# Keeping the residual stream token-major, and multiplying the output weights as the moving operand

## The reference, cut to what matters

```python
h = h + rmsnorm(mixer(rmsnorm(h, g0)), g1)          # layers 0 and 1
h = h + rmsnorm(conv_ffn(rmsnorm(h, g2)), g3)
x = x + 0.5 * swiglu(rms_norm(x, n1))                # second block
x = x + concat(mla, moba) @ w_out                    # on rms_norm(x, n2)
x = x + 0.5 * swiglu(rms_norm(x, n3))
return rms_norm(x, final)

def rmsnorm(x, g):
    return x * rsqrt(mean(x * x, axis=-1) + 1e-6) * g
def conv_ffn(x, w_up, conv_w, conv_b, w_down):
    h = causal_dwconv(x @ w_up, conv_w, conv_b)      # 2 x 2816 channels
    return (gelu(h[..., :2816]) * h[..., 2816:]) @ w_down
```

## Time and profile before

| | before |
|---|---|
| median of three runs | 1165.03 us |
| span of the profiled execution | 1165.7 us |
| TensorE busy (matmul) | 1113.5 us, 96% |
| TensorE weight load busy | 1084.9 us, 93% |
| VectorE busy | 810.1 us, 69% |
| ScalarE busy | 621.9 us, 53% |
| GpSimd busy | 68.5 us, 6% |
| read from HBM | 188.58 MB, 164 GB/s over the span |

### The profile page before, as it was taken

The page is one execution under the profiler, slowest core; times in us unless marked ns, Lnnn a source line. Parts: engine busy times, 40 slices in busy tenths (PEclk is TensorE's granted clock), DMA queues, the critical chain, the costliest instruction groups (busy, mean ns, idle before and its releaser), DMA issues.

```text
span 1165.7 us, 23900 instructions
## 1 busy us (share of the span) xinstructions
PE 1113.5 (96%) x8840; PEld 1084.9 (93%) x8840; DVE 810.1 (69%) x1245; ACT 621.9 (53%) x1048; POOL 68.5 (6%) x79
## 2 busy tenths in 40 slices
PE   6798999999899889999998999999999999999996
PEld 5698999999799889999998999999999999999995
DVE  5587887776858768877777755655766868656554
ACT  5455655555646656655555644444554656444442
POOL 0077000000200001000001000000000000000000
PEclk9899999999999999999999999999999999999998
DMA  9763565555353243655554465565552435565630
GB/s 335 151 227 113 167 212 180 180 180 180 106 181 129 91 163 99 212 180 193 180 180 146 147 191 186 172 190 178 160 165 92 152 113 171 184 194 165 193 111 36
DMA packets 54033, 191.91 MB, mean 165 GB/s; under 512 B 6504, under 2 KB 6920, under 8 KB 53984
## 3 DMA queue, kind: packets, MB, share of 16 engines
q1 hardware_dynamic: 52272, 187.96, 49.5%
q0 software_dynamic: 1088, 2.63, 1.4%
q10 hardware_dynamic: 624, 0.64, 0.2%
HBM read 188.58 MB, written 2.62 MB: 164 GB/s over the span
## 4 chain that ended last, share of the span: by engine, by line
PE 87%; DVE 6%; DMA 4%; ACT 2%; issue 1%; POOL 0%; SPq 0%; DVEq 0%; ACTq 0%; POOLq 0%
PE G L1127 18%; PE G L1128 18%; PE G L1129 18%; PE Y L1127 8%; PE Y L1129 8%; PE Y L1128 8%; DMA raw<-in_panels 4%; DVE w_low L666 1%; PE PB L1144 1%; PE Y L1185 1%; PE Y L1187 1%; PE Y L1186 1%; ACT w_high L349 1%; PE PB L1290 1%; DVE rbc L677 1%
## 5 line engine op out<-in xcount | busy, mean ns | idle before, releaser
L1127 PE MATMUL G<-x_high,w_high 128*128 128x256 f32 x1712 | 489.1, 286 | 8.8 <-DVE x_low L684 8.8
L1128 PE MATMUL G<-x_low,w_high 128*128 128x256 f32 x1712 | 485.8, 284 | 0.0
L1129 PE MATMUL G<-x_high,w_low 128*128 128x256 f32 x1712 | 485.7, 284 | 0.0
L666 DVE TENSOR_TENSOR w_low<-raw,w_high 128x1024 fp32r<-128x1024 f32 x352 | 428.1, 1225 | 57.3 <-ACT w_high L349 56.8
L349 ACT CAST w_high<-raw 128x1024 fp32r<-128x1024 f32 x352 | 363.3, 1042 | 94.6 <-PE G L1129 65.5
L1127 PEld LDWEIGHTS G<-x_high,w_high 128*128 128x128 f32 x1712 | 329.9, 193 | 11.1 <-issue 9.6
L1128 PEld LDWEIGHTS G<-x_low,w_high 128*128 128x128 f32 x1712 | 330.0, 193 | 0.2
L1129 PEld LDWEIGHTS G<-x_high,w_low 128*128 128x128 f32 x1712 | 330.0, 193 | 0.0
L1127 PE MATMUL Y<-a_high,w_high 128*128 128x256 f32 x896 | 255.5, 285 | 0.0
L1128 PE MATMUL Y<-a_low,w_high 128*128 128x256 f32 x896 | 254.2, 284 | 0.0
L1129 PE MATMUL Y<-a_high,w_low 128*128 128x256 f32 x896 | 254.1, 284 | 0.0
(11 more groups left out here) (201 smaller groups left out, 889.5 us busy)
## 6 DMA issues: line engine op xcount, KB each, us to landing
raw<-in_panels SPq DMA_DIRECT2D x352, 512.0 KB, 3.7
rel_rows<-qk POOLq DMA_DIRECT2D x1, 1536.0 KB, 34.9
h<-in_x SPq DMA_DIRECT2D x4, 256.0 KB, 10.1
bias<-rel_rows POOLq DMA_DIRECT2D x8, 128.0 KB, 4.4
out_y<-big SPq DMA_DIRECT2D x4, 256.0 KB, 2.0
big<-in_w_s SPq DMA_DIRECT2D x1, 512.0 KB, 12.5
wc<-in_b_s SPq DMA_DIRECT2D x1, 512.0 KB, 13.9
cst<-in_consts ACTq DMA_DIRECT2D x1, 320.5 KB, 5.5
```

Of the source, the lines that this page charges most:

```text
L666: v.tensor_tensor(WL[:, j, :], raw[:, j, :], WH[:, j, :].bitcast(F32), ALU.subtract).then_inc(lo, 1)
L1127: mm(out, WH[:, j, c:c + w], xh, start=first, stop=False, skip_group_check=skip)
L1128: mm(out, WH[:, j, c:c + w], xl, start=False, stop=False, skip_group_check=skip)
L1129: return mm(out, WL[:, j, c:c + w], xh, start=False, stop=last, skip_group_check=skip)
```

## The change

The kernel is written anew around another layout. What it does:

1. `h`, the stage's output and all norms are token-major: 128 tokens on the partitions and 1024 features side by side, for token tile 0 and token tile 1. The sum of squares of a token is then one pass of ScalarE with its accumulator, and the reciprocal root is one number on each partition. The sums with a matrix of ones (1144) are gone, and so is the multiplication of the tiles by the norm (`rbc`), since x is normalised before it is used. The gains are rows now, spread over the partitions by DMAs: one of 512 KB at each boundary, two at boundaries 1 to 4.
2. x has to be turned back to feature-major for the products. TensorE transposes it in 128 x 128 blocks, 16 at each of the stages' starts (`turn_x`), ScalarE and VectorE write the high and low part from there.
3. An output panel keeps a 128-token block of the hidden activations stationary and moves 512 weight columns (`rows`): 12 matmuls, six for each token tile.
4. The last five output panels of a stage (`tail`) serve token tile 0 first, save that one part of tile 1 is put in; the boundary's work on tile 0 begins while TensorE still works on tile 1 of the other four.
5. The first four feature tiles of a stage (`first_tiles`, boundaries 1, 3, 4, 5 and 6) are computed for token tile 0 and then for token tile 1, with 128 moving columns each. The first value panels (the start and boundary 2) serve tile 0, then tile 1, with 512 moving columns as before.
6. The raw ring has five buffers, that of high and low parts eight. Six matmuls without use (`warm`) stand before `turn_x` at each of boundaries 1 to 6. The loops are unrolled. In feed-forward stages the accumulator banks of the gate and up tiles are four instead of two, and the convolution reads them there.
7. At the start, the LayerNorm statistics of token tile 1 and the offset are computed behind more panel splits, the mixing comes at the seventh panel of the second product instead of the fifth, and the DMAs that read the attention bias back come later.

```diff
-RING = 6
+RAWS = 5
+RING = 8
-            def rows_into_y(n, j, xh, xl, first, last):
-                ready(n)
-                for k in range(KT):
-                    end = product(Y[:, k, :], j, k * P, P, xh, xl, first and k % 2 == 0, last, skip=True)
+            def rows(n, slot, t, first, last):
+                ready(n)
+                j = n % RING
+                xh, xl = AH[:, slot, tok(t)], AL[:, slot, tok(t)]
+                for x, w, start, stop in ((xh, WH, first, False), (xl, WH, False, False), (xh, WL, False, last)):
+                    for c in range(2):
+                        end = mm(Y[:, 2 * t + c, :], x, w[:, j, half(c)], start=start, stop=stop)
+                if t == 1:
+                    end.then_inc(used, 1)
...
+            def turn_x(b, t):
+                for c in range(2):
+                    pe.wait_ge(xn_r, quarter(b, t, c))
+                    for j in range(4):
+                        last = nc.tensor.transpose(Y[:, 2 * t + c, j * P:(j + 1) * P],
+                                                   xn[:, t, (4 * c + j) * P:(4 * c + j + 1) * P], ident)
+                    last.then_inc(xt_r, 1)
+            def tail(end, slots, before=None):
...
+                for i in range(4):
+                    part(i, 0)
+                part(0, 1)
+                part(4, 0).then_inc(y_done, 1)
+                for i in range(1, 4):
+                    part(i, 1)
+                part(4, 1)
+            def first_tiles(b, outs):
+                n = STARTS[b]
+                turn_x(b, 0)
+                for m in range(3):
+                    tile_part(b, n + m, outs[m], 0)
+                turn_x(b, 1)
+                tile_part(b, n + 3, outs[3], 0)
+                for m in range(4):
+                    tile_part(b, n + m, outs[m], 1)
```

The boundary on VectorE, for boundaries 1 to 4 and for the others:

```diff
+                if b in POST:
+                    y_scale(b, 0)
+                    link(y_normed(b, 0, 0))
+                    link(y_normed(b, 0, 1))
+                    h_add(0, 0), h_add(0, 1)
+                    half_mean(b, 0)
+                    upto(base + 4)
+                    x_normed(b, 0)
+                    y_scale(b, 1)
+                    link(y_normed(b, 1, 0))
+                    x_low(b, 0, 0)
+                    link(y_normed(b, 1, 1))
+                    x_low(b, 0, 1)
+                    h_add(1, 0), h_add(1, 1)
+                elif b:
+                    h_plus_y(b, 0)
+                    half_mean(b, 0)
+                    x_normed(b, 0)
+                    if b < 7:
+                        x_low(b, 0, 0), x_low(b, 0, 1)
+                    h_plus_y(b, 1)
+                half_mean(b, 1)
+                x_normed(b, 1)
```

More of the change, by code:

```diff
@@ L42 @@
 REL = 384
[L45 removed]
+WARM = 6
 GMLP = 0
@@ L269, in _ @@
+            for t in range(TT):
+                for c in range(2):
+                    sp.wait_ge(out_r, 2 * t + c + 1)
+                    sp.dma_start(io["out"][tok(t), half(c)], xn[:, t, half(c)]).then_inc(out_sem, 16)
             sp.wait_ge(out_sem, 64)
@@ L432, in ffn @@
+                if not conv:
+                    gap(2)
+                gap(1)
             def ffn(ph, base, with_conv):
-                def static(f):
-                    def split_next(c):
-                        if 6 < 3 * f + c and base + 3 * f + c < PANELS:
-                            splits(base + 3 * f + c, base + 3 * f + c)
+                for f in range(NF):
                     c0 = C_CONV + (ph * NF + f) * 8
-                    hidden(f % 2, ph * NF + f + 1,
-                           (lambda c: par[:, c0 + c:c0 + c + 1]) if with_conv else None, split_next,
-                           (used, base + 3 * f + 1), f == NF - 1)
@@ L458, in ffn @@
-                for f in range(2 + 2 * turns, NF):
-                    static(f)
+                    hidden(ph, base, f, (lambda c, c0=c0: par[:, c0 + c:c0 + c + 1]) if with_conv else None)
+                preload(ACT.Sqrt)
+                upto(base + 3 * NF + 3)
             def exps(a):
@@ L519, in _ @@
-            high_s(4), high_s(5)
             gate_u(3)
-            high_s(6), high_s(7)
-            splits(20, 22)
+            for k in range(4, KT):
+                high_s(k)
+            upto(23)
             act.wait_ge(ang_r, 1)
@@ new lines, in half_mean, with x_normed @@
+            def half_mean(b, t):
+                dve.wait_ge(h_sq0, 2 * b + t + 1)
+                v.tensor_scalar(bt[:, t:t + 1], ss2[:, t, 0:1], 1.0 / D, EPS, ALU.mult, ALU.add).then_inc(bt_r, 1)
+            def x_normed(b, t):
+                dve.wait_ge(h_std, 2 * b + t + 1)
+                link(v.reciprocal(rs2[:, t:t + 1], sd2[:, t:t + 1]))
+                if t == 0 and b:
+                    dve.wait_ge(gn_in, 16 * b)
+                elif t == 0:
+                    dve.wait_ge(gain_ps, 1)
+                for c in range(2):
+                    gain = gN[:, half(c)] if b else G[:, 2 + c, :]
+                    v.scalar_tensor_tensor(out=xn[:, t, half(c)], in0=h[:, t, half(c)], scalar=rs2[:, t:t + 1],
+                                           in1=gain, op0=ALU.mult, op1=ALU.mult)\
+                        .then_inc(xn_r if b < 7 else out_r, 1)
@@ new lines, in hidden @@
+                last.then_inc(pr, 1)
+                if not conv:
+                    gap(2)
+                gap(1)
+                dve.wait_ge(hh, i + 1)
+                v.tensor_tensor(AL[:, slot, :], wc[:, pf, 1, 0:T], AH[:, slot, :].bitcast(F32), ALU.subtract)\
+                    .then_inc(hl, 1)
+            def ffn(ph, base, with_conv):
+                for f in range(NF):
+                    c0 = C_CONV + (ph * NF + f) * 8
+                    hidden(ph, base, f, (lambda c, c0=c0: par[:, c0 + c:c0 + c + 1]) if with_conv else None)
+                upto(base + 3 * NF + 3)
```

1042 lines of the change are left out of this document (497 added, 545 removed).

## The result

The changed kernel takes 1219.68 us, the median of four runs (1201.78 to 1227.05), against 1164.47 us before. It is slower by the factor 1.0388, 95% interval 1.0318 to 1.0458. The forecast was 1173 us and slower, with a range of 1143 to 1215. By the factor (about 1210 us) the time lies inside the range, near its slow end; the median of all four lies just outside, and so do three of the four runs. The profiled execution has 1227.05 us with a span of 1224.9, so against the span before (1165.7) there are 59.2 us to find.

What follows compares the result with a forecast made beforehand. The prediction took TensorE's own cadence to bound the stages, with the rest lost at boundaries and in the first stage. Its terms summed to +7.9 us on the 1165.0 us median, giving 1173 us, range 1143 to 1215.

Steps and rivals of the forecast that it cites:

- the floor of the short product: First tiles: a 128-column product takes 0.107 us, a floor that doesn't depend on the columns.
- a sign of being wrong: First tiles: the forecast is wrong if the granted clock is low there.
- Output panels: 112 panels go from 24 matmuls of 0.120 us to 12 of 0.227, 0.156 each: -17.5 us.
- First tiles: At five boundaries 96 matmuls of 256 columns become 192 of 128 at 0.107 us: +9.0 each, +45.1 in all.
- the cheap rival: A 128-column product of rounded parts takes 0.067 us, five boundaries give back 38 us: 1135 us; chance 0.14.
- Transposes: Boundaries 1 to 6: eight of 16 transposes stand on the path, 0.86 us each boundary, +5.1 us.
- Waits: TensorE waits 4.05 us at boundaries 1, 3, 4 (-20.6); boundary 2 -7.0; boundaries 5, 6 3.4 each (+1.7).
- End: From last output matmul to last output block, 4.4 us instead of 10.8: -6.4 us.
- Tails: Thinner cover in stage tails: +2 us differential attention, +3 last four MLA pairs, +1.5 two convolution stages.
- Start: First stage: the stall moves forward and stays about as long, -1 us, between -8 and +6.
- Clock: Longer waits in the tails can lower TensorE's clock: +2 us allowed.
- The dear rival: 128-column product costs 0.213 to 0.223 us, by a fallen clock or plain float32 passes: 1275 to 1284 us; chance 0.16.

Runs made afterwards that it cites:

- first stage mended and the clock kept up: Changed kernel with matmuls without use in the boundaries' idle places and the row write behind the first stage's mixing: 1175.59 us; kernel before with its row write moved: 1153.48.
- experiment above: Changed kernel with matmuls without use in the boundaries' idle places, its last five output panels served panel by panel, both token tiles each: 1219.17 us, ratio 1.0452.
- filled gaps: Changed kernel with matmuls without use in the idle places of every boundary after the first stage: 1195.24 us, ratio 1.0267 to the kernel before.
- short tiles inside a stage: Changed kernel with the last four feature tiles of each feed-forward stage in two halves of 128 columns, without idle time ahead: 1259.23 us.
- two other kernels: Changed kernel with only the row write moved behind the first stage's mixing, 1205.01 us; changed kernel with each feed-forward stage's last four feature tiles in halves, 1259.23 us.
- the tiles served whole: Changed kernel with the first four tiles at boundaries 1 and 3 to 6 served whole, after all 16 transposes: 1189.94 us, ratio 1.0222.
- two tiles in halves: Changed kernel with boundary idle places filled and row write moved, only two of the first four tiles at boundaries 1 and 3 to 6 in halves: 1198.87 us.

## Why the prediction was right and wrong

The direction was right, and so was the mechanism that carried the sum, the floor of the short product. With the first stage mended and the clock kept up the kernel is still slower (+22 us), so the direction doesn't hang on the clock. The size was wrong: +8 forecast, +55 measured by the medians and +45 by the factor. That the factor stays inside the range is luck: what fills the distance, clock and start, is not what the range was drawn for. And the granted clock was low in the first tiles, which the prediction itself had named as a sign of being wrong. Step by step:

- **Output panels**: -17.5 forecast. A feed-forward stage became 3.2 us shorter where the step had 22 x 0.156 = 3.4. Right.
- **First tiles**: +45.1 forecast at 0.107; measured 0.112 at full clock, which is +10.0 a boundary and +50. The number that was to decide lay inside 0.10 to 0.12, and the cheap rival (0.067) fell. By the Trainium skill ("TensorE: Matmul & The Clock Gate", section "Back-to-back issue gap") it would have been 81 ns; the trace, with 112, doesn't agree.
- **Transposes**: 0.86 forecast, 0.82 measured.
- **Waits**: 4.05 forecast for boundaries 1, 3 and 4; measured 4.87, 4.03 and 4.02. 3.4 for boundaries 5 and 6; measured 3.43 and 3.42. The 4.05 is a chain of 9.5 us less its cover; the order of the tail changes the chain as well (experiment above), so the agreement holds for this order alone. Boundary 2 missed by 2.7: the sum left out two table loads that ScalarE runs ahead of its square, which moving lambda's exponential showed. The 1.0 us forecast there for token tile 1's transposes did not come; TensorE has no idle place ahead of them.
- **End**: -6.4 forecast, -6.5 measured.
- **Tails**: differential attention +2 forecast and +2.1 measured (0.8 plus the 1.25 that its eight output panels gain), but up to 1.7 of it is clock (6.8 us low against 3.4), which the sum had elsewhere. Mixed attention +3 forecast and 5.8 measured; its waits in the last pair (2.54 and 0.66 us) came as counted, and I hadn't counted the 6.8 us low behind them, up to 3.4. The 1.5 us for the two convolution stages did not come: all output panels together waited 0.3 us for their hidden activations.
- **Start**: -1, with +6 as the far end; measured +10.3, and 11.6 without the gain of its eight output panels. This step failed first. I put both kernels' stall down to the order of VectorE's work and the late panel 13, and didn't ask why it was late. The row write, 36 us on its way, holds up the panels issued behind it (21 us to land instead of 5.5, by the median). In the changed kernel 9 panels were split ahead of that, not 12, and the offset needs panels 11 and 12. Moving the write brought the stage's end 19.9 us forward here and 11.6 in the kernel before; one buffer more did nothing.
- **Clock**: +2; measured 69 us more at the low clock than before, worth about 35 in the profiled execution, some 29 of them at the boundaries, and 24 of 55 in the medians (1219.7 to 1195.2 by filling). This is the step that made the size wrong. The sum had the idle time at each boundary and let "much of it filled" stand for all of it. Idle places of 1.02 to 1.06 us remained, with a second one of 0.84 at boundary 1 alone, and behind them the clock fell at four of the five boundaries with short products. The dear rival had the right price (0.213) but the wrong cause: it let dense short products bring the clock down, and they don't (filled gaps; short tiles inside a stage). What follows the fall differs, though. With 256-column products the clock was back within some 5 us of their start at every boundary looked at; with 128-column products it stayed low for 13.6 to 17.0 us in the changed kernel, and for 44.4 us in three stretches of two other kernels, with 177 to 179 of the 192 products in them.

With start (12.6, its panels' gain left out), clock at the boundaries (27 above the 2), short product (5), boundaries 1 and 2 (2.5) and mixed attention (3), less 1.5 for the convolution stages, the 8 us of the sum become some 56, of 59.2 found.

The Trainium skill's section "HAM oscillation — how this bites in real kernels" ("TensorE: Matmul & The Clock Gate"), cited in the prediction, tells of waits of 3 to 5 us between bursts. These runs agree that idle gaps between bursts can cost the clock, and show it with shorter ones, of 1.02 to 1.40 us; filling them gave back 24 and 37 us.

Open: why an idle place of about 1 us brings a fall at one boundary and not at another, and why the low stretches behind short products end after 13.6 us in some executions and not in 39 in others. At boundaries 1, 3, 4 and 5 of the profiled run the return (130.9, 468.8, 677.0 and 885.2) falls 0.5 to 1.8 us behind the last of token tile 1's eight transposes, and so it does at boundary 4 of the run with the moved write; in the three stretches of 44.4 us the same transposes bring nothing. No run tells. Nor is it shown what a boundary without short products and without idle time would cost, since token tile 1's chain leaves some 7 us to cover.

## What to carry to other kernels

Sum a boundary twice: once in waits and once in clock, since a gap of 1 to 1.4 us on TensorE, with short products behind it, can cost 6 to 20 us (an estimate from 56 to 177 products at 0.213 instead of 0.112); put a few matmuls without use into every such gap before judging a change. Halving the moving columns from 256 to 128 saves next to nothing per product here (0.112 against 0.120 us) and doubles their number, so use split tiles only as long as they cover a wait. If a panel is late, ask what large transfer was issued ahead of it, and move that to where panels may be late.

## What the hardware showed that I had not expected

- At the low clock a product with 128 columns takes as long as one with 256, 0.213 us from start to start (the changed kernel at boundary 1, and in the first stage at 256 columns), while at full clock they have 0.112 and 0.120:

```profile
119.94 0.41 PE L1120 MATMUL G<-x_parts,w_high 128*128 128x128 f32 x1
...
120.58 0.41 PE L1120 MATMUL G<-x_parts,w_high 128*128 128x128 f32 x1
```

```profile
49.47 0.41 PE L1120 MATMUL Y<-x_parts,w_high 128*128 128x256 f32 x1
...
50.11 0.41 PE L1120 MATMUL Y<-x_parts,w_high 128*128 128x256 f32 x1
```

- Low time costs by what runs in it. With the tiles served whole, 91 us were low, but the six tiles behind each gap took only 1.3 to 2.1 us longer than 17.28; with two tiles in halves, 82 of 97 us were low at boundaries and cost 37.
- One 1.5 MB transfer from another queue was 36 us on its way, and the median way of the 512 KB panels from issue to landing was 21.0 us beside it and 5.5 without.
